# Heads 2 to 7 of a recurrent decoder step: the decode states times queries as rounded two-column products at a later place

## The reference

```python
# decode samples: T = 1, the state s_in comes from 8192 earlier tokens
f  = lb + (1 - lb) * sigmoid(fpre)         # (DK,)
S  = f[:, None] * s_in + (1 - f)[:, None] * v[None, :]   # (DK, DV), an output too
o  = S.T @ silu(q)                         # (DV,)
oA = o * rsqrt(mean(o*o) + eps) * o_norm * silu(g)
```

## Time and profile before

| | us |
|---|---|
| Median of three runs | 2422.62 (2420.93 to 2422.63) |
| The profiled execution, its own time | 2422.87 |
| Its span in the trace | 2421.1 |
| PE busy | 2407.1 (99%) |
| PEld busy | 2393.6 (99%) |
| DVE busy | 1742.5 (72%) |
| ACT busy | 1324.8 (55%) |
| POOL busy | 211.1 (9%) |
| Share of PE in the chain that ended last | 95% |
| Granted clock of TensorE, mean over the span | 0.999 |

### The profile page before, as it was taken

The page is one execution under the profiler, slowest core; times in us unless marked ns, Lnnn a source line. Parts: engine busy times, 40 slices in busy tenths (PEclk is TensorE's granted clock), DMA queues, the critical chain, the costliest instruction groups (busy, mean ns, idle before and its releaser), DMA issues.

```text
span 2421.1 us, 51609 instructions
## 1 busy us (share of the span) xinstructions
PE 2407.1 (99%) x19250; PEld 2393.6 (99%) x19250; DVE 1742.5 (72%) x2853; ACT 1324.8 (55%) x2253; POOL 211.1 (9%) x245
## 2 busy tenths in 40 slices
PE   9999999999999999999999999999999999999998
PEld 8999999999999999999999999999999999999998
DVE  8867777677689888887768776443587777777776
ACT  5555555555558666676666664221455555555554
POOL 1111111111120000000000000000301111111113
PEclk9999999999999999999999999999999999999999
DMA  5555555555541343333322235432225555555556
GB/s 197 123 123 122 122 122 122 122 122 122 132 186 54 92 110 89 88 98 90 113 96 87 70 123 184 151 125 94 88 68 124 123 122 123 121 122 122 121 123 202
DMA packets 139622, 286.80 MB, mean 118 GB/s; under 512 B 67328, under 2 KB 71936, under 8 KB 139008
## 3 DMA queue, kind: packets, MB, share of 16 engines
q1 hardware_dynamic: 114176, 192.39, 24.3%
q0 software_dynamic: 25344, 93.01, 20.4%
HBM read 159.02 MB, written 123.22 MB: 117 GB/s over the span
## 4 chain that ended last, share of the span: by engine, by line
PE 95%; DVE 2%; ACT 1%; DMA 1%; POOL 1%; issue 0%; DVEq 0%; ACTq 0%; POOLq 0%
PE banks L157 30%; PE banks L158 30%; PE banks L159 30%; POOL n_sumsq L286 1%; PE banks L1895 1%; PE banks L1930 1%; PE banks L1917 1%; PE banks L1934 0%; DMA x_sum<-f_snap 0%; PE banks L1928 0%; DMA raw<-w_slabs 0%; DVE x L1141 0%; DVE f_blk_f L540 0%; DVE f_blk_lo L564 0%; PE banks L500 0%
## 5 line engine op out<-in xcount | busy, mean ns | idle before, releaser
L157 PE MATMUL banks<-f_blk_hi,f_u_hi 128*128 128x258 f32 x2496 | 706.7, 283 | 0.9 <-ACT f_snap L940 0.4
L158 PE MATMUL banks<-f_blk_lo,f_u_hi 128*128 128x258 f32 x2496 | 705.7, 283 | 0.0
L159 PE MATMUL banks<-f_blk_hi,f_u_lo 128*128 128x258 f32 x2496 | 704.8, 282 | 0.0
L157 PE MATMUL banks<-mix_blk_hi,mix_u_hi 128*128 128x258 f32 x1808 | 513.7, 284 | 0.4 <-ACT mix_snap L1479 0.3
L158 PE MATMUL banks<-mix_blk_lo,mix_u_hi 128*128 128x258 f32 x1808 | 511.3, 283 | 0.0
L159 PE MATMUL banks<-mix_blk_hi,mix_u_lo 128*128 128x258 f32 x1808 | 510.1, 282 | 0.0
L157 PEld LDWEIGHTS banks<-f_blk_hi,f_u_hi 128*128 128x128 f32 x2496 | 471.4, 189 | 2.7 <-issue 1.3
L159 PEld LDWEIGHTS banks<-f_blk_hi,f_u_lo 128*128 128x128 f32 x2496 | 471.2, 189 | 0.0
L158 PEld LDWEIGHTS banks<-f_blk_lo,f_u_hi 128*128 128x128 f32 x2496 | 470.9, 189 | 0.2
L157 PEld LDWEIGHTS banks<-mix_blk_hi,mix_u_hi 128*128 128x128 f32 x1808 | 342.0, 189 | 1.6 <-issue 0.8
L158 PEld LDWEIGHTS banks<-mix_blk_lo,mix_u_hi 128*128 128x128 f32 x1808 | 341.4, 189 | 0.2
(11 more groups left out here) (320 smaller groups left out, 4248.3 us busy)
## 6 DMA issues: line engine op xcount, KB each, us to landing
raw<-w_slabs SPq DMA_DIRECT2D x220, 512.0 KB, 3.4
x_sum<-f_part POOLq DMA_DIRECT2D x140, 516.0 KB, 7.8
x_sum<-f_snap POOLq DMA_DIRECT2D x20, 516.0 KB, 10.2
x<-x_sum SPq DMA_DIRECT2D x16, 516.0 KB, 8.4
sg_kept<-sgt SPq DMA_DIRECT2D x8, 1032.0 KB, 5.7
sgs<-sg_kept SPq DMA_DIRECT2D x16, 516.0 KB, 4.5
x_sum<-x_t POOLq DMA_DIRECT2D x8, 516.0 KB, 6.9
x_kept<-x SPq DMA_DIRECT2D x1, 4128.0 KB, 12.1
```

Source lines behind the costliest of these rows:

```text
L157: pe.matmul(out, wh, xh, start=start, stop=False, skip_group_check=chained)
L158: pe.matmul(out, wh, xl, start=False, stop=False, skip_group_check=chained)
L159: return pe.matmul(out, wl, xh, start=False, stop=stop, skip_group_check=chained)
```

## The change

The decode product of heads 1 to 6 counted from 0 (the six turns of the loop, "heads 2 to 7" counted from 1) is done with rounded operands.

- ACT, at half 7, copies the 8 query columns to `sample_q[:, :, 0]` in rounded form and four states to `ss_hi`; at half 10 the other four states (`split_high`).
- POOL has a loop over the six heads (`split_gpsimd`) that subtracts the rounded parts from the full values, for the queries (8 columns) and for the states (twice 512 columns), into `sample_q[:, :, 1]` and `ss_lo`. Two semaphores of the first norm are used again for its signals.
- PE no longer does the eight float32 matmuls at half 10. After half 12 (`split_tensor`) it does 16 rounded matmuls, for each sample one with `ss_hi` and one with `ss_lo` as weights, and with both columns of `sample_q` as the moving operand. Each gives two columns, which are added up in PSUM over the two weights.
- DVE at half 12 adds each sample's two columns into `qe` (`split_sum`, a `tensor_reduce`) in place of the copy L2102, and its copy L2100 at half 10 waits for the prompt outputs alone.
- On ACT, the second sigmoid on `f` stands ahead of `finish_square` and `finish_high`, no longer behind them.
- Three SBUF tiles are placed in regions that the second half of the mixer uses.

```diff
+HIGH_BASE, LOW_BASE = 13 - 3, 11 - 3
+
+def split_high(act, k, s, h, part):
+    if part == 0:
+        act.wait_ge(s.qe_ready, h * 1 + 1)
+        act.wait_ge(s.o_ready, h * 9)
+        act.activation(s.sample_q[:, :, 0], s.qe[:, SEQ:T], ACT.Copy).then_inc(s.ss_high, 1)
+        act.wait_ge(s.v_moved, h * (2 * MOVED) + 2 * MOVED)
+    four = slice(4 * part, 4 * part + 4)
+    act.wait_ge(s.ss_new, h * 8 + 4 * (part + 1))
+    act.activation(s.ss_hi[:, four, :], s.ss[:, four, :], ACT.Copy).then_inc(s.ss_high, 1)
+
+def split_gpsimd(pool, k, s):
+    with pool.Fori(1, HEADS - 1) as h:
+        pool.wait_ge(s.ss_high, h * 3 + (HIGH_BASE + 1))
+        pool.tensor_tensor(s.sample_q[:, :, 1], s.qe[:, SEQ:T], s.sample_q[:, :, 0].bitcast(F32), ALU.subtract)\
+            .then_inc(s.ss_low, 1)
+        for part in range(2):
+            four = slice(4 * part, 4 * part + 4)
+            pool.wait_ge(s.ss_high, h * 3 + (HIGH_BASE + 2 + part))
+            pool.tensor_tensor(s.ss_lo[:, four, :], s.ss[:, four, :], s.ss_hi[:, four, :].bitcast(F32), ALU.subtract)\
+                .then_inc(s.ss_low, 1)
+
+def split_tensor(pe, k, s, h):
+    pe.wait_ge(s.o_used, h * 9 + 8)
+    for b in range(DEC):
+        if b in (0, 4):
+            pe.wait_ge(s.ss_low, h * 3 + (LOW_BASE + 2 + b // 4))
+        out = k.bank[7][:, 2 * P + 2 * b:2 * P + 2 * b + 2]
+        pe.matmul(out, s.ss_hi[:, b, :], s.sample_q[:, b, :], start=True, stop=False, skip_group_check=True)
+        last = pe.matmul(out, s.ss_lo[:, b, :], s.sample_q[:, b, :], start=False, stop=True, skip_group_check=True)
+    last.then_inc(s.o_ready, 1)
+
+def split_sum(dve, k, s, h):
+    dve.wait_ge(s.o_ready, h * 9 + 9)
+    pairs = k.bank[7][:, 2 * P:2 * P + 2 * DEC].rearrange("p (b two) -> p b two", two=2)
+    dve.tensor_reduce(s.qe[:, SEQ:T], pairs, mybir.AxisListType.X, ALU.add).then_inc(s.o_used, 1)
...
@@ core_tensor
-        if a == 4:
+        if a == 4 and not split:
             pe.wait_ge(s.ss_new, h * 8 + 8)
             for b in range(DEC):
                 last = pe.matmul(k.bank[7][:, 2 * P + b:2 * P + b + 1], s.ss[:, b, :], s.qe[:, SEQ + b:SEQ + b + 1],
                                  start=True, stop=True, skip_group_check=True)
-        last.then_inc(s.o_ready, 3 if a == 4 else 2)
+        last.then_inc(s.o_ready, 3 if a == 4 and not split else 2)
...
@@ paired_core_vector
-        dve.wait_ge(s.o_ready, h * 9 + (9 if a == 4 else 2 * a))
+        dve.wait_ge(s.o_ready, h * 9 + (9 if a == 4 and not split else 2 * a))
...
-    if a == 4:
+    if a == 4 and not split:
         dve.tensor_copy(s.qe[:, SEQ:T], k.bank[7][:, 2 * P:2 * P + DEC]).then_inc(s.o_used, 1)
...
@@ mid_tensor, beside_core
+            if kind == HGRN and not first and half == 12:
+                split_tensor(pe, k, s, j - 1)
...
@@ mid_scalar, core_pair
+            if hf in (7, 10) and kind == HGRN and not first:
+                split_high(act, k, s, h, (7, 10).index(hf))
             if hf == 12:
                 if kind == HGRN:
                     shape(j, 0, 1, s.f[:, half(1)], ACT.Sigmoid, s.shaped)
+                    shape(j, 0, 2, s.f[:, half(0)], ACT.Sigmoid, s.shaped)
                     if not first:
                         finish_square(act, k, s, h)
                         finish_high(act, k, s, h)
-                    shape(j, 0, 2, s.f[:, half(0)], ACT.Sigmoid, s.shaped)
...
@@ mid_vector, core_pair
+            if hf == 12 and kind == HGRN and not first:
+                split_sum(dve, k, s, h)
...
@@ gpsimd
             norm_gpsimd(pool, k, nm, range(NT - 1))
+            split_gpsimd(pool, k, w)
             lru_gpsimd(pool, k, w)
```

More of the change, by code:

```diff
@@ L1884, in core_tiles, with core_tensor @@
     return [n for n in (2 * a - 1, 2 * a) if 0 <= n < TILES]
-def core_tensor(pe, k, s, h, a):
+HIGH_BASE, LOW_BASE = 13 - 3, 11 - 3
[31 more added lines that the diff above has]
+    dve.tensor_reduce(s.qe[:, SEQ:T], pairs, mybir.AxisListType.X, ALU.add).then_inc(s.o_used, 1)
+def core_tensor(pe, k, s, h, a, split):
     def scores():
@@ L2092, in first_core_vector, with paired_core_vector @@
         dve.copy_predicated(s.sc[:, n % 2, :], k.mask[:, 0, :], k.bank[5][:, 0:P]).then_inc(s.sc_used, 1)
-def paired_core_vector(dve, k, s, h, a):
+def paired_core_vector(dve, k, s, h, a, split):
     if a:
-        dve.wait_ge(s.o_ready, h * 9 + (9 if a == 4 else 2 * a))
+        dve.wait_ge(s.o_ready, h * 9 + (9 if a == 4 and not split else 2 * a))
         dve.tensor_copy(s.qe[:, (2 * a - 2) * P:2 * a * P], k.bank[7][:, 0:2 * P]).then_inc(s.o_used, 2)
-    if a == 4:
+    if a == 4 and not split:
         dve.tensor_copy(s.qe[:, SEQ:T], k.bank[7][:, 2 * P:2 * P + DEC]).then_inc(s.o_used, 1)
@@ L2109, in paired_core_vector, with core_vector @@
                             k.mask[:, :, :].rearrange("p a b -> p (a b)"), k.bank[5][:, 0:2 * P]).then_inc(s.sc_used, 2)
-def core_vector(dve, k, s, h, n, first=False):
+def core_vector(dve, k, s, h, n, first, split):
     if first:
@@ L2115, in core_vector @@
     elif n in CORE_STEPS:
-        paired_core_vector(dve, k, s, h, CORE_STEPS.index(n))
+        paired_core_vector(dve, k, s, h, CORE_STEPS.index(n), split)
     if n == 3:
@@ L2402, in beside_core @@
             if not first and half - 1 in CORE_STEPS:
-                core_tensor(pe, k, s, j - 1, CORE_STEPS.index(half - 1))
+                core_tensor(pe, k, s, j - 1, CORE_STEPS.index(half - 1), kind == HGRN)
+            if kind == HGRN and not first and half == 12:
+                split_tensor(pe, k, s, j - 1)
         def beside_lru(half):
@@ L2592, in core_pair @@
         for hf in range(1, 13):
-            core_vector(dve, k, s, h, hf - 1, first)
+            core_vector(dve, k, s, h, hf - 1, first, kind == HGRN and not first)
             if hf == 1 and not first:
@@ L3344, in build @@
     k.mid.kt = r.put("kt", [P, TILES, P], F32)
+    k.mid.sample_q = r.put("sample_q", [P, DEC, 2], F32R)
+    k.mid.ss_lo = Region(xr, gates_at).put("ss_lo", [P, DEC, P], F32R)
+    k.mid.ss_hi = Region(gates_at + 4128, end).put("ss_hi", [P, DEC, P], F32R)
     k.mid.sgt = Region(gates_at, end).put("sgt", [P, 2, T], F32)
@@ L3412, in build @@
                   norm=nm, gate_up_done=f1.prod, down_used=f1.down_used, ffn_unit_lo=f1.unit_lo, **k.mid)
+        w.ss_high, w.ss_low = n1.squared, n1.squared_vector
         w.oa_loaded, w.ob_loaded = x_loaded[:4], x_loaded[4:]
```

## The result

The changed kernel takes **2431.34 us** (median of six runs, 2431.15 to 2431.55), the kernel before 2422.47 us (six runs, 2420.93 to 2424.05). The ratio is 1.0039, with an interval of 1.0028 to 1.0049: slower by 8.9 us. The forecast was 2433.2 us, range 2426 to 2437. The profiled execution took 2431.15 us, its span 2429.4 us.

The account below looks back on a forecast made before the run. PE's own work (busy 99%) was taken as the bound and unchanged; three new waits of 1.16, 0.30 and 0.28 us make 1.74 us a turn, six turns 10.4 us, giving 2433.2 us, range 2426 to 2437.

Parts of the forecast that it names:

- PE's work doesn't change: Decode product on PE: 16 rounded matmuls at 0.112 us take 1.79 us, as the 8 float32 ones (16 rows) did.
- The signal is late by 2.54 us: Product moved behind half 12: the new sum starts at 878.65, so ACT's square at 878.84 instead of 876.30.
- The sigmoid gives back 0.52 us: ACT: moving the second sigmoid ahead of the square cuts the lateness behind the rounded squares from 2.54 to 2.02 us.
- Wait 1: PE at product 1 of pair 1 waits 1.16 us for ACT's `take`, ending at 883.97; margin before 0.86 us.
- Waits 2 and 3: PE waits for DVE's late mixes: 0.30 us at product 6 of pair 1, 0.28 at product 0 of the next group.
- DVE's mixes with some 3.5 us: Sign of being right: PE's list of waits shows DVE's mixes with some 3.5 us.
- The sum: PE's three waits, 1.16 + 0.30 + 0.28, make 1.74 us a turn; six turns make 10.4 us.
- What was to be free: Means, ACT's three split copies and POOL's subtractions fit without delay; POOL's second subtraction runs from about 874.1 to 876.2.
- cheap loads: Rival: rounded loads on PE cost 0.06 us a matmul, -0.8 us a turn, waits remaining: 2428.2 us; chance 0.15.
- no wait: Rival: ACT's chain finds room ahead of the square or margins exceed 2 us, so PE's work alone counts: 2422.9; chance 0.10.
- the faster side: Rival: rounded loads at 0.06 us and `take` in time: 2417.6 us; chance 0.08.
- POOL's block: Rival: DVE stands still for a whole POOL instruction, delaying half 8's state steps for PE's half 10: 2436.2 us; chance 0.05.

Follow-up runs that it names:

- e5: Changed kernel without the eight products with ss_lo (8 matmuls instead of 16 a turn): 2426.83 us, ratio 1.0022.
- e9: Changed kernel with the second sigmoid on f put back behind the squares on ACT: 2434.73 us, ratio 1.0051.
- e1: Changed kernel with the float32 product and its copy at half 12, no split on ACT and POOL, sigmoid still moved: 2432.32 us, ratio 1.0042.
- e7: Changed kernel with the split kept but unused, the old float32 product at half 10, the second sigmoid behind the squares: 2421.97 us, ratio 0.9999.
- e4: Changed kernel with weight 5's rounded part and the silu on q ahead of the square on ACT: 2421.76 us, ratio 0.9999.

## Why the prediction was right

The sign, the place and the mechanism were right, and the sum was 1.9 us too high. Step by step:

- **PE's work doesn't change**, 16 rounded rows at 0.112 us: measured 1.79 us, to the digit, with e5's count near it. Why it came out so well: the price was read where one rounded load follows a short product, the nearest row there was.
- **The signal is late by 2.54 us**: the sum began at 878.63 (forecast 878.65), the square at 878.84 (878.84).
- **The sigmoid gives back 0.52 us**: e9 shows 0.52 a turn. `take` began at 883.38, where 883.39 was expected.
- **Wait 1, 1.16 us**: 1.27 us. `take` ended at 883.96, as forecast; the margin was read wrongly. I measured it to the start of the matmul at 882.81, but the wait stands ahead of its weight load, and that load came one pace, 0.12 us, earlier. The true margin was 0.74 us. The loads of the kernel before, at product 1, product 6 and product 0 of the next group:

```profile
882.69 0.19 PEld L157 LDWEIGHTS banks<-mix_blk_hi,mix_u_hi 128*128 128x128 f32 x1
898.04 0.19 PEld L157 LDWEIGHTS banks<-mix_blk_hi,mix_u_hi 128*128 128x128 f32 x1
900.92 0.19 PEld L157 LDWEIGHTS banks<-mix_blk_hi,mix_u_hi 128*128 128x128 f32 x1
```

- **Waits 2 and 3, 0.30 and 0.28 us**: this term was mis-sized. They are 0.07 and 0.24, together 0.31 (0.29 as PE's rows have it, the distance from the means to the transposes). The steps that failed are that the first weight sum moves by the same 2.02 us, and "from there to the end of pair 1 DVE has no idle time that would take this up". The first weight sum began at 886.21, not 886.39: the slab landed 3.7 us after its issue instead of 3.9, and DVE's idle time ahead of the sum was 1.00 instead of 1.17 us. And over the next 12 us DVE caught up another 0.12 us. Its mixes were 1.7 us late, not 2.02, and where margins are this small 0.3 us is half of the term. The sign "DVE's mixes with some 3.5 us" failed with it: the list has 0.9, and the stops are 2.6 us over the six turns. The turn read is a mild one: the others lost 0.31 to 0.64 us at the two mixes.
- **The sum**: 1.27 + 0.31 = 1.58 us in this turn, 1.67 on average over the loop, against 1.74; 10.0 us against 10.4. Errors of 0.11 and -0.27 partly cancelled, and not by luck. A wait that PE has already made pushes back its need for the next signal, so the three together are the lateness of the last mix less the margin there. The forecast has 2.02 - 0.28 = 1.74. Measured are 1.68 us of lateness and 0.11 of margin (the load at 900.92, the mix done at 900.76, and 0.05 from the end of a mix to the load that waited for it), or 1.57. What was wrong at `take` came back at the mixes; both the lateness and the last margin had been put too high. The medians differ by 8.9 us in the first comparison and the loops of two traces by 10.0; the start of the mixer, which varies by more than 1 us from trace to trace, is enough for that difference.
- **What was to be free was free.** POOL's second subtraction ran from 874.23 to 875.66 (expected from 874.1 to 876.2 at the latest), and nobody waited for it; e1 and e7 show it in the time.

The rivals: cheap loads fell by the distance and by e5; no wait and the faster side fell by the six waits. The room ahead of the square on which "no wait" would have rested does exist, as e4 shows; but the order of ACT's list has to be written so. The rival of POOL's block needs a correction. I wrote that the trace shows delays of 0.3 us, not a full stop. The timeline of POOL in the changed kernel:

```profile
868.39 1.74 POOL L1911 TENSOR_TENSOR ss_lo<-ss,ss_hi 128x512 fp32r<-128x512 f32 x1 [0.81 <-ACT ss_hi L1899]
874.23 1.43 POOL L1911 TENSOR_TENSOR ss_lo<-ss,ss_hi 128x512 fp32r<-128x512 f32 x1 [4.10 <-ACT ss_hi L1899]
```

DVE's state step L2121 at 874.75 took 1.05 us, where it had taken 0.34 us. It ended at 875.80, just behind POOL's end at 875.66: it stood still until POOL was done. That agrees with the Trainium skill (SBUF — State Buffer, Who interferes with whom), which says that a DVE instruction with two SBUF inputs contends with a GpSimd instruction that reads SBUF, and calls the shared port pair an exclusive lock. The block cost nothing here, for another reason than the one that I gave: DVE had 1.63 us of idle time two instructions later, before the sum. Where DVE is the late one the same subtraction could cost what is left of it when DVE's instruction starts, 0.7 us here; no run shows that case.

What stays open: the varying start of the mixer, why the stops at product 6 differ from kernel to kernel (1.1 to 1.8 us with the waits for `take` alike), and a product with the queries as weights and the states as the moving operand, which was not tried.

## What to carry to other kernels

On an engine that is busy for 99%, work that is moved later costs nothing on that engine itself, but every signal that it gives comes later; so list, for each engine behind the signal, the margin of the first thing that PE wants from it, counted to PE's weight load (0.74 us here, for a move of 2.54). A late signal does its harm through what is queued behind its waiter, and the order there is right for one place of the signal only: the same exchange of two ACT instructions was worth +9 us with the product at half 10 and -3 us with it at half 12. A short product cost its weight loads here, float32 or rounded; fewer matmuls saved time, another type of operand didn't. And where one late chain makes PE wait several times, the waits don't add up freely: the last one, its lateness less its margin, gives the sum.

## What the hardware showed that I had not expected

- A DVE instruction with two SBUF operands beside a POOL instruction with two was held until POOL's ended: 1.05 us instead of 0.34. The state step at 869.81, started 0.3 us before the end of POOL's first subtraction (870.13), took 0.47 us: the same hold, met near its end. Beside all 12 subtractions the state step ended 0.14 to 0.16 us behind POOL. The copy of 256 columns from PSUM, inside the same subtractions, took its usual 0.42 us.
- The idle time printed at a weight load is less than what the stop costs: 1.21 us was printed for 1.27 lost, and nothing for the 0.07 at product 6, since a load's row lasts 0.19 us where loads follow each other at 0.12. So the 0.9 us that the list has for the mixes is less than their share, 2.6 us; the longer stops at product 6 stand in the list as "issue".
- POOL took 1.41 to 1.74 us for the same subtraction of 512 columns, by what ran beside it: each started while a DVE instruction with two SBUF operands was running, and each ended 1.14 to 1.16 us behind the end of that one. The hold seems to work both ways.
